# One opening stage by token tile with moved rotary tables, and norms joined to the expert tails

## The reference

```python
x = x + hier_moe(rms_norm(x, g_moe), ...)
x = rms_norm(x, g_final)                       # "the final norm" of the first layer
alpha = (2.0 * DEPTH_2) ** 0.25
for l in range(2):
    mix = _token_mixer(x, positions, ...)
    x = _layernorm(alpha * x + mix, ln1_g[l], ln1_b[l])
    ffn = _hier_moe(x, ...)
    x = _layernorm(alpha * x + ffn, ln2_g[l], ln2_b[l])
return x
# rms_norm: x * rsqrt(mean(x*x) + eps) * g;  _layernorm: (x - mean) * rsqrt(var + eps) * g + b
```

## Time and profile before

| | us |
|---|---|
| three runs, median | 2988.84 |
| lowest, highest | 2984.93, 2992.25 |
| the profiled execution, its time | 2988.36 |
| its span | 2986.6 |
| TensorE busy | 2446.4 (82%) |
| DVE busy | 1301.6 (44%) |
| ScalarE busy | 896.1 (30%) |
| GpSimd busy | 405.7 (14%) |
| opening, up to the first transpose | 0 to 36.8 |
| first expert stage's last matmul to the first token mixer's transposes | 1084.2 to 1117.2 |
| second expert stage's last matmul to the second token mixer's transposes | 2010.7 to 2053.5 |
| third expert stage's last matmul to the end | 2930.6 to 2986.6 |

### The profile page before, as it was taken

How to read it: one execution, slowest core, us unless ns; L and a number is a source line. 1 busy time by engine, 2 the same in 40 slices (tenths; PEclk the granted TensorE clock), 3 DMA queues, 4 the chain that set the end, 5 groups by cost and what they waited for, 6 DMA issues and landing times. The chain is left out here.

```text
span 2986.6 us, 50527 instructions
## 1 busy us (share of the span) xinstructions
PE 2446.4 (82%) x18120; PEld 1916.5 (64%) x18121; DVE 1301.6 (44%) x2778; ACT 896.1 (30%) x1690; POOL 405.7 (14%) x718
## 2 busy tenths in 40 slices
PE   4996799698889759699898879984959989869882
PEld 4985698554445438576677867754847767857661
DVE  4466335421112136545554543335734844453334
ACT  2534333221111113245433223322233633223221
POOL 1000000121212110000000144441000000024343
PEclk9999899799999979899999889997979999969996
DMA  3201235599999934122113479974112212459993
GB/s 126 89 1 57 90 94 200 204 406 406 411 409 402 399 132 130 36 60 56 48 51 92 174 283 394 380 285 164 43 53 62 62 51 65 157 228 381 373 388 135
DMA packets 209305, 565.80 MB, mean 189 GB/s; under 512 B 26598, under 2 KB 170598, under 8 KB 184592
## 3 DMA queue, kind: packets, MB, share of 16 engines
q1 hardware_dynamic: 191104, 538.73, 48.7%
q0 software_dynamic: 18064, 25.23, 2.6%
HBM read 560.46 MB, written 36.18 MB: 200 GB/s over the span
## 5 line engine op out<-in xcount | busy, mean ns | idle before, releaser
L1031 PE MATMUL ps<-m_gate_up,e_xT 128*64 128x256 f32 x1088 | 270.8, 412 | 62.9 <-DMA m_gate_up<-in_w_gate_up 52.8
L1031 PEld LDWEIGHTS ps<-r_gate_up,e_xT 128*64 128x64 f32 x2272 | 260.3, 141 | 84.9 <-issue 82.2
L1031 PE MATMUL ps<-r_gate_up,e_xT 128*64 128x128 f32 x2272 | 272.2, 280 | 36.4 <-DMA r_gate_up<-in_w_exp_gate_up 25.5
L1185 DVE TENSOR_TENSOR e_hid<-e_silu,ps 64x128 f32<-64x128 f32 (+1 forms) x210 | 70.2, 335 | 477.7 <-ACT e_silu L1073 461.1
L1031 PEld LDWEIGHTS ps<-m_gate_up,e_xT 128*64 128x64 f32 x1088 | 160.3, 149 | 175.3 <-issue 111.6
L1033 PE MATMUL ps<-r_gate_up,e_xT 128*64 128x128 f32 x2272 | 272.3, 280 | 0.0
L1033 PE MATMUL ps<-m_gate_up,e_xT 128*64 128x256 f32 x1088 | 270.8, 412 | 0.0
L1073 ACT ACTIVATE e_silu<-ps 64x128 f32<-64x128 f32 (+1 forms) x210 | 63.6, 303 | 656.2 <-PE ps L1033 623.3
L1033 PEld LDWEIGHTS ps<-r_gate_up,e_xT 128*64 128x64 f32 x2272 | 260.3, 141 | 0.0
L2286 PE MATMUL ps<-t_hT,t1a_t1g_w 128*128 128x512 f32 x768 | 198.4, 409 | 4.6 <-DVE t1a_t1g_w L2308 2.4
L2286 PE MATMUL ps<-t_hT,t0a_t0g_w 128*128 128x512 f32 x768 | 198.3, 409 | 4.6 <-DVE t0a_t0g_w L2308 2.4
(11 more groups left out here) (649 smaller groups left out, 4781.1 us busy)
## 6 DMA issues: line engine op xcount, KB each, us to landing
m_gate_up<-in_w_gate_up SPq DMA_DIRECT2D x32, 4096.0 KB
r_gate_up<-in_w_exp_gate_up SPq DMA_DIRECT2D x64, 2048.0 KB
m_down<-in_w_down SPq DMA_DIRECT2D x32, 2048.0 KB
r_down<-in_w_exp_down SPq DMA_DIRECT2D x64, 1024.0 KB
t0a_t0g_raw<-in_w_in SPq DMA_DIRECT2D x32, 512.0 KB, 3.8
t1a_t1g_raw<-in_w_in SPq DMA_DIRECT2D x32, 512.0 KB, 3.8
mixw_raw<-in_w_in SPq DMA_DIRECT2D x10, 1024.0 KB, 5.2
xaw_raw<-in_w_kv_x SPq DMA_DIRECT2D x8, 1024.0 KB
```

The lines of the kernel that those rows point to most:

```text
L1031: nc.tensor.matmul(ps_gu[q][0:SLOTS], xT[:, c, :], ring.gu[s][:, 0, c, span], start=c == 0, stop=c == DC - 1)
L1185: vec.tensor_tensor(hid[SLOTS:P, q], silu[SLOTS:P, q], ps_gu[q][SLOTS:P], ALU.mult).then_inc(hid_ready, 1)
```

## The change

1. *Opening.* The small stages become one, `start_up`. SP issues x as four loads of one token tile, then the columns, then all small rows, the positions and the first mixer's small matrices, and waits for all of them at the end. GpSimd writes all constants and masks beside it (`make_constants`). DVE takes the statistics of a tile as it lands, ScalarE takes the root and scales the tile.
2. *Rotary tables.* Class `Rope`: the ten DVE operations run in the cross attention's projections after chunk 0, the two sines on ScalarE after chunk 1.
3. *Norms.* `final_norm` and `post_norm` go. In the tail of `moe` the normalization without gain and bias is done by token tile: the second add of a tile also sums it (layer norms), ScalarE squares the centred tile with a sum, DVE and ScalarE make the factors, ScalarE rescales x in place.
4. *Gains and biases.* For the next mixer they are applied twice: per feature in its `TurnSplit` (g_final as a factor; for the second layer norm factor and bias, with the spare tile `merged` between), and as rows on x in `project_route` before the residual add (`residual`). The rows lie in `merged` after it has been split, and so do those of the first layer norm, so SP waits for that split before it loads them. After the third expert stage the rows are loaded among the values that come back, and DVE multiplies and adds; each tile is stored as it is done.

The core of the diff:

```diff
@@ class TurnSplit, high (ScalarE) and low (DVE)
+        if self.bias is None:
+            self.nc.scalar.activation(high, self.bank(c), ACT.Identity, scale=scale).then_inc(self.high_ready, 1)
+            return
+        if c % 2 == 1:
+            act.wait_ge(self.whole_ready, c // 2 + 1)
+            self.nc.scalar.copy(high, self.spare[:, c, :]).then_inc(self.high_ready, 1)
+            return
+        bias = self.bias[:, c:c + 1]
+        self.nc.scalar.activation(high, self.bank(c), ACT.Identity, scale=scale, bias=bias).then_inc(self.high_ready, 1)
+        act.wait_ge(self.high_ready, c + 1)
+        self.nc.scalar.activation(self.spare[:, c, :], high, ACT.Identity, scale=-1.0, bias=bias).then_inc(self.away_ready, 1)
...
+        if self.bias is not None and c % 2 == 1:
+            dve.wait_ge(self.high_ready, c + 1)
+            vec.tensor_tensor(low, self.spare[:, c, :], high, ALU.subtract).then_inc(self.low_ready, 1)
+            return
+        if self.bias is not None:
+            n = c + 1
+            dve.wait_ge(self.full, n + 1)
+            vec.tensor_scalar(self.spare[:, n, :], self.bank(n), self.factor[:, n:n + 1], self.bias[:, n:n + 1], ALU.mult,
+                              ALU.add).then_inc(self.whole_ready, 1)
+            dve.wait_ge(self.away_ready, c // 2 + 1)
+            vec.scalar_tensor_tensor(low, self.bank(c), self.factor[:, c:c + 1], self.spare[:, c, :], ALU.mult,
+                                     ALU.add).then_inc(self.low_ready, 1)
+            return
@@ start_up
+                for t in range(TT):
+                    sp.dma_start(x[:, t, :], rows_of_x[t * P:(t + 1) * P]).then_inc(x_landed[t], 16)
+                sp.dma_start(columns[:], column_rows).then_inc(columns_landed, 16)
+                for dst, src in loads:
+                    sp.dma_start(dst, src).then_inc(late_landed, 16)
+                sp.wait_ge(late_landed, 16 * len(loads))
...
+                def squares(t):
+                    at = slice(t, t + 1)
+                    dve.wait_ge(x_landed[t], 16)
+                    for q in range(D // 256):
+                        last = vec.bn_stats(stats[:, t, q, :], x[:, t, q * 256:(q + 1) * 256])
+                    link(last)
+                    link(vec.bn_aggr(mv[:, t, :], stats[:, t]))
+                    link(vec.scalar_tensor_tensor(r[:, 3, at], mv[:, t, 0:1], mv[:, t, 0:1], mv[:, t, 1:2], ALU.mult, ALU.add))
+                    vec.tensor_scalar(r[:, 0, at], r[:, 3, at], 1e-6, None, ALU.add).then_inc(mean_ready, 1)
...
+                for t in range(TT):
+                    act.wait_ge(mean_ready, t + 1)
+                    sca.activation(r[:, 1, t:t + 1], r[:, 0, t:t + 1], ACT.Sqrt).then_inc(root_ready, 1)
+                    act.wait_ge(factors_ready, t + 1)
+                    sca.activation(h[:, t, :], x[:, t, :], ACT.Identity, scale=r[:, 2, t:t + 1])
@@ moe, SP
+                    if norm.out is not None and t == 0:
+                        for n in range(2):
+                            sp.dma_start(norm_rows[:, n], norm.rows[n].partition_broadcast(P)).then_inc(norm_rows_landed, 16)
+                if norm.out is not None:
+                    for t in range(TT):
+                        sp.wait_ge(finished, t + 1)
+                        sp.dma_start(norm.out[t * P:(t + 1) * P], x[:, t, :]).then_inc(out_stored, 16)
@@ moe, ScalarE
+                square(0)
+                for t in range(TT):
+                    act.wait_ge(mean_ready, t + 1)
+                    sca.activation(added[:, 3, t:t + 1], added[:, 3, t:t + 1], ACT.Sqrt).then_inc(root_ready, 1)
+                    if t + 1 < TT:
+                        square(t + 1)
+                    rescale(t)
@@ moe, DVE
+                def finish(t):
+                    if norm.out is not None:
+                        dve.wait_ge(normed, t + 1)
+                        if t == 0:
+                            dve.wait_ge(norm_rows_landed, 32)
+                        link(vec.tensor_tensor(x[:, t, :], x[:, t, :], norm_rows[:, 0], ALU.mult))
+                        vec.tensor_tensor(x[:, t, :], x[:, t, :], norm_rows[:, 1], ALU.add).then_inc(finished, 1)
+
+                add(0, 0)
+                add(0, 1)
                 for t in range(TT):
...
+                    if t + 1 < TT:
+                        add(t + 1, 0)
+                    mean(t)
+                    if t + 1 < TT:
+                        add(t + 1, 1)
+                    factors(t)
+                    if t:
+                        finish(t - 1)
+                finish(TT - 1)
@@ project_route
                 if finish is not None:
+                    sp.wait_ge(before.low_ready, before.n)
+                    for n, r_ in enumerate(residual[1]):
+                        sp.dma_start(residual[0][:, n], r_.partition_broadcast(P)).then_inc(residual_landed, 16)
...
+                    if residual is not None:
+                        if i == 0:
+                            dve.wait_ge(residual_landed, 16 * len(residual[1]))
+                        for r_, op in zip(range(len(residual[1])), (ALU.mult, ALU.add)):
+                            link(vec.tensor_tensor(xs, xs, residual[0][:, r_, c * WIDTH:(c + 1) * WIDTH], op))
                     dve.wait_ge(bank_full, i + 1)
```

More of the change, by code:

```diff
@@ L1256, in _, with __init__ @@
                     pool.wait_ge(rows_gathered[n], n_pairs * 16 + 32 - 16 * n)
+class Norm:
+    def __init__(self, centre, eps, columns, rows, out=None):
+        self.centre, self.eps, self.columns, self.rows, self.out = centre, eps, columns, rows, out
 class Columns:
@@ L1986, in token_mixer @@
+def token_mixer(nc, name, k, x, col, i, l, router, ring, row, norm):
     ps, vec, sca = k["ps"], nc.vector, nc.scalar
@@ L2217, in token_mixer @@
                       lambda t: x[:, t, :], turned_rows, col(f"ln1_g{l}"), col(f"ln1_b{l}"),
-                      finish=(finish, row(f"ln1_g{l}"), row(f"ln1_b{l}")))
+                      finish=(spread[:, 2:4], row(f"ln1_g{l}"), row(f"ln1_b{l}")), residual=(spread, norm.rows))
 class GatedBranches:
```

357 lines of the change are left out of this document (163 added, 194 removed).

## The result

The changed kernel took 2940.12 us (median of four runs, 2938.64 to 2941.11) against 2989.99 for the kernel before (four runs): a ratio of 0.9835, 95% interval 0.9821 to 0.9849, 49.9 us less. The forecast was 2939 in a range of 2928 to 2952. The profiled execution has a span of 2936.8 us where the kernel before had 2986.6.

What follows compares the result with a forecast made beforehand. TensorE or the expert-weight stream sets the pace except in four gaps without matrix work, each its own chain. Terms -20.4 - 6.8 - 15.7 + 2.8 - 10.8 + 1.4 = -49.5 from 2988.8 give 2939 us, range 2928 to 2952.

Steps and rivals of the forecast that it cites:

- Opening: Before the first matmul: one joined stage brings the first transpose at 16.4 us instead of 36.75, 20.4 us less.
- The bound for GpSimd's selections: Opening: DVE's statistics held by GpSimd's mask selections, from nothing to 4.4 us; taken as nothing.
- Rope tables: Cross attention's projections: the moved DVE operations and sines fit in idle time, nothing on the path; 1.8 us without this cover.
- First tail: After the first expert loop: norm by token tile, 7.1 us less; the factor in the next split costs 0.3; 6.8 less net.
- Second tail: After the second expert loop: layer norm by token tile without GpSimd, 15.7 us less; bias split adds 2.8.
- The bias split: Second mixer's start: norm's gain and bias in the split delay the first item by 2.8 us, bounds 0.5 to 5.
- End: After the third expert loop: late rows delay tile 1 by 4.1 us, then DVE is the bound; 10.8 us less.
- the larger-gain rival: Late rows at the end cost nothing, the split overlaps, less waiting: 2932 us; chance 0.05.
- Residual: Both output projections: the last tile's product waits for GpSimd's addition, 1.4 us more for both, bounds 0 and 4.
- A held opening: Opening held by its own loads (some 4 us) or GpSimd's selections (up to 4.4), not both in full: 2945 us; chance 0.13.
- DVE-bound tails: Tails: DVE's one-column operations and waits cost 0.1 us more each, bias split at its upper bound: 2947 us; chance 0.15.
- The slower case: Mixers: late residual rows stall TensorE; a 30 us delay in each would end at 2999 us; chance 0.01.

Runs made afterwards that it cites:

- the two halves: Kernel before with only the new opening and moved rope tables, 2976.66 us; kernel before with only the new tails, bias split and residual rows, 2961.14 us.
- the repeat: The changed kernel profiled and run again without an edit: 2942.36 us, ratio 0.9833 against the kernel before.

## Why the prediction was right, point by point

**What bounds it.** Right. The gaps are four chains of their own, and the two halves add up.

**Opening**, -20.4 forecast, -20.0 measured. Tile 0 was there at 4.57 (4.6), a tile took DVE 2.11 us (2.3), the exit 0.8 (1.1). One step was missed: ScalarE scales tile 2 before it takes the root of tile 3, so the root is at 14.41 where DVE had been ready since 13.24. Of that 1.2 us, tiles, exit and last pass, each somewhat shorter than forecast, gave back 0.8. The bound for GpSimd's selections was 0 to 4.4 and I took 0: statistics beside a selection took 1.41 for four and 1.39 alone. Only the small operation at 6.31, with two operands in SBUF, took 0.47 instead of 0.22; it ended at 6.78, with GpSimd's selection (5.84 and 0.93). The Trainium skill, "SBUF — State Buffer", section "Who interferes with whom", says that a DVE instruction with two SBUF inputs contends with a GpSimd instruction that reads SBUF, and that one with at most one such input, outside the two-port modes, does not. The trace agrees, with 0.25 us, less than the 0.3 that I had drawn from it as the least. The late loads held nothing either: no transfer runs after 15.0, and ScalarE's last pass ends at 15.97.

**Rope tables**, 0. The chain took DVE 2.4 us (342.69 to 345.07) and ScalarE 1.8, both in waits of those engines. From the first to the last matmul of the cross attention's projections it is 90.1 to 90.2 us in nine of the eleven profiles with the moved tables (92.8 in the other two), against 89.8 and 89.9 in the two with the tables unmoved. So they seem to cost 0.3, which the forecast had at nothing; no run has the tables as its only edit.

**First tail**, -6.8 forecast, -7.7 and +0.3. The gap is 24.5 to 25.5 in all eleven profiles with the new tail against 33.0 and 33.3 in the two with the old, somewhat better than the 26. The split's 0.3 was right: the first item is copied 12.9 to 13.2 us after the first transpose in nine profiles against 12.8. The 14.08 of the first profile of the changed kernel and 13.8 of another don't repeat; in the former ScalarE waits 0.89 us for the first weights there.

**Second tail**, -15.7 and +2.8 forecast. The gap is as said, 27.1 (26.4 to 28.2 in eleven profiles), though two of its pieces missed and cancel: from the first add to the end of the last DVE took 12.5 us (13.0), the last tile 4.4 (4.3), the exits 1.8 (1.4). The sum inside an add costs DVE a row of 0.08, taken as 0 within 0 to 0.19:

```profile
2002.94 0.08 DVE L1257 DVE_READ_ACCUMULATOR all_x<-r_gate_up,e_weight,all_x 128x1 f32 x1
```

The bias split was played through right to its first matmul (8.7 against 8.62) and at the first item (2.8 against 3.0), but I stopped there. The second item is late by 3.5 in most profiles. That term was mis-sized by 0.7, within its bounds of 0.5 to 5: not by the split, which costs 2.4 there where the clock stays up, but by TensorE's clock, which falls after the pause that the split makes and which the forecast had left out.

**End**, -10.8 forecast, -12.4 measured: the largest error, in four pieces. The rows delay tile 1 by 3.8 (4.1). DVE's chain from there takes 19.5 (21): the waits among its one-column operations, which I had added up, are mostly covered by the long operations in between (a tile of the second tail took DVE 3.04 us, 0.4 and not 0.8 more than two adds). The last store and the end take 4.6 (3.85). And the first add came 12.0 us after the last expert's rows were copied, not 12.4. The gain taken for the larger-gain rival, that the rows cost nothing, fell.

**Residual**, +1.4 forecast with bounds of 0 and 4, 1.6 to 2.2 measured. A product takes 0.42 to 0.44 us and not the 0.35 that I had scaled down from 1024 columns, but outside the last tile that is off the path. The hold came as forecast: the last add starts 2.4 and 2.9 us behind the projection's last matmul in the repeat, against 0.9 before, so it is 1.5 and 2.0 late (1.6 and 2.0). What was over-counted is the share of it that the transposes and the router's queue hide, 1.3 to 1.9 and not 2.2 of some 3.5. The mechanism was right in both its parts. The rows were there 18.6 us after the stage's start (17.9 forecast); DVE then worked without a break, and TensorE went on through the items without a wait:

```profile
2536.58 45.38 PE L1802 MATMUL ps<-t1o_w,t_hT 128*128 128x256 f32 x360 [9.48 <-DVE t1o_w L1899]
...
2547.91 0.89 DVE L1913 TENSOR_TENSOR all_x<-all_x,t_merged 128x256 f32<-128x256 f32 x2 [4.95 <-DMA t_merged<-in_rows]
...
2555.25 2.29 DVE L1904 TENSOR_TENSOR t1o_w<-t1o_raw,t1o_w 128x2048 fp32r<-128x2048 f32 x1
```

The split of chunk 2, the last row, ends 28.2 us after the stage's start (26.9 forecast) and was needed at 30.2 (eight items of 2.87 behind the first matmul), so of the 3 us to spare 2 were there. The product of the last tile waited for GpSimd as said.

**The rivals.** A held opening is excluded: 0.25 us for GpSimd, nothing for the loads. DVE-bound tails: its small operations cost less than I gave them, not more. The slower case needed rows 30 us late; they were 0.7 late.

**The sum** was right to 0.3 us, which is luck beyond the terms' own precision: errors of +0.4, -0.6, +0.7, -1.6 and +0.2 to +0.8 nearly cancel, and the third expert stage began 6 us later in the second profile than in the first, of which the two gaps ahead of it make 0.7. The medians, 49.9 and 50.2 us apart in two series, say that the sum holds apart from that.

## What to carry to other kernels

Look first for stretches in which the engine that bounds the kernel does nothing, and price what is in them as a chain from its own start; gains of separate gaps add. In such a chain count for each engine what is queued ahead of the step on the path, as ScalarE's scaling of the tile before is here. Operands that a tail needs belong in the queue before its stage's last loads, and in a tail like this GpSimd should have no work beside DVE instructions that read two SBUF operands, nor be the last to work. A pause of TensorE can cost more than its length: where the clock fell behind one here, the next item took up to 0.8 us longer.

## What was not expected of the hardware

- An instruction of GpSimd as the last of the program put 3.1 us more between the loop and the end, even with one element; behind it, as behind four additions, 8.0 us lay until the end instead of 4.6 behind DVE's last. Why is open.
- Behind a pause of 2.2 to 3.5 us TensorE's granted clock fell to 0.50 in eight of ten profiles of the same stretch and stayed at 1.00 in two.
- An unedited kernel, profiled twice, had the same 32 matmuls at 3.66 and 6.88 us, and its third expert stage at places 6 us apart, while its median of five runs was 2.2 us from that of four other runs.
- DVE and GpSimd both lose when they overlap on operands in SBUF: 1.28 became 3.18 for the one and 2.35 became 3.21 for the other, so that moving 4.9 us of work away from the engine that sets the pace made the chain 3.4 us longer.
